# First chunks of the weight stream in another order: two modulation chunks ahead of the first query chunk

## What is computed

```
mod = silu(c) @ w_mod + b_mod                      # shift1, scale1, gate1, shift2, scale2, gate2
h   = rmsnorm(x, g_norm1) * (1 + scale1) + shift1  # c for latent tokens, c_ctx for context tokens
proj = h @ w_in + b_in                             # q, k, v, o, gates, pooling and branch gate columns
x  += gate1 * W_out(sig(g_a) * P_a(mLSTM(h)) + sig(g_b) * P_b(pool(h)))
x  += gate2 * HierMoE(h2)                          # 4 groups of 4 experts, top 1 group, top 2 experts
y   = rmsnorm(x, g_final)
```

## Time and profile before

| | us |
|---|---|
| median of 3 runs | 987.95 (986.37 to 990.32) |
| the profiled execution's own span | 983.7 |
| TensorE busy | 948.3 (96% of the span) |
| VectorE busy | 599.8 (61%) |
| ScalarE busy | 476.2 (48%) |
| GpSimd busy | 123.2 (13%) |

### The profile page before, as it was taken

One profiled execution on the slowest core, in us unless ns is written; L12 is line 12 of the kernel. 1 busy time (PEld: TensorE's weight loads), 2 busy tenths in 40 slices (PEclk: granted clock), 3 DMA queues, 4 the chain that ended last, 5 costly groups with the idle time before them and its releaser, 6 DMA issues.

```text
span 983.7 us, 13956 instructions
## 1 busy us (share of the span) xinstructions
PE 948.3 (96%) x5638; PEld 836.6 (85%) x5638; DVE 599.8 (61%) x767; ACT 476.2 (48%) x638; POOL 123.2 (13%) x133
## 2 busy tenths in 40 slices
PE   2999999999999999999999999989999999999986
PEld 1788888789999999999999998877888888888862
DVE  5353210234788862321344555459999999999998
ACT  5542121223566643122341242255878778787863
POOL 0000000001110029950000000002112111111100
PEclk9999999999999999999999999989999999999998
DMA  9835454713433253242212218148999999999964
GB/s 379 314 122 213 171 208 171 278 53 96 126 105 99 65 226 129 86 172 76 71 59 86 86 51 334 61 153 318 421 420 414 423 419 408 422 418 411 396 275 168
DMA packets 36192, 219.02 MB, mean 223 GB/s; under 512 B 3968, under 2 KB 4160, under 8 KB 15648
## 3 DMA queue, kind: packets, MB, share of 16 engines
q1 hardware_dynamic: 26496, 180.25, 46.5%
q0 software_dynamic: 8768, 35.15, 10.2%
q10 hardware_dynamic: 864, 2.73, 0.7%
HBM read 200.70 MB, written 17.42 MB: 222 GB/s over the span
## 4 chain that ended last, share of the span: by engine, by line
PE 90%; DMA 4%; DVE 4%; ACT 1%; issue 1%; SPq 0%; DVEq 0%; POOLq 0%; ACTq 0%
PE ps L1703 85%; PE ps L1759 2%; PE ps L2171 1%; DMA h2scr<-ht 1%; DMA xT<-in_x 1%; PE ps L2199 1%; DMA raw<-in_wst 1%; PE ps L1748 1%; DMA xg<-h2scr,slot_rows 0%; PE ps L2018 0%; PE ps L1911 0%; DVE rowA L1658 0%; DVE xr L1661 0%; DVE xr L1665 0%; DMA rowB<-yscr 0%
## 5 line engine op out<-in xcount | busy, mean ns | idle before, releaser
L1026 DVE TENSOR_TENSOR wlo<-raw,whi 128x2048 fp32r<-128x2048 f32 x29 | 67.5, 2327 | 158.4 <-ACT whi L633 158.4
L1703 PE MATMUL ps<-hhi,whi 128*128 128x320 f32 x672 | 155.5, 313 | 0.0
L1703 PE MATMUL ps<-hhi,wlo 128*128 128x320 f32 x672 | 153.1, 309 | 0.0
L1703 PE MATMUL ps<-hlo,whi 128*128 128x320 f32 x672 | 153.0, 309 | 0.0
L1703 PEld LDWEIGHTS ps<-hhi,whi 128*128 128x128 f32 x672 | 111.9, 188 | 11.3 <-ACT QK L680 5.9
L1703 PEld LDWEIGHTS ps<-hlo,whi 128*128 128x128 f32 x672 | 112.4, 188 | 0.0
L1703 PEld LDWEIGHTS ps<-hhi,wlo 128*128 128x128 f32 x672 | 112.3, 188 | 0.0
L633 ACT ACTIVATE whi<-raw 128x2048 fp32r<-128x2048 f32 x29 | 55.4, 1911 | 103.7 <-PE ps L1703 62.5
L1514 DVE TENSOR_TENSOR olo<-raw,ohi 128x2048 fp32r<-128x2048 f32 x32 | 72.4, 2288 | 3.9 <-ACT ohi L930 3.9
L1514 DVE TENSOR_TENSOR wlo<-raw,whi 128x2048 fp32r<-128x2048 f32 x31 | 70.3, 2289 | 5.0 <-ACT whi L930 4.7
L930 ACT ACTIVATE whi<-raw 128x2048 fp32r<-128x2048 f32 x32 | 61.3, 1918 | 18.8 <-PE ps L1703 18.8
(11 more groups left out here) (380 smaller groups left out, 1993.6 us busy)
## 6 DMA issues: line engine op xcount, KB each, us to landing
raw<-in_wexp SPq DMA_DIRECT2D x64, 1024.0 KB, 9.5
raw<-in_wst SPq DMA_DIRECT2D x60, 1024.0 KB, 5.1
eraw<-in_wexp SPq DMA_DIRECT2D x32, 1024.0 KB, 8.1
nm<-negscr POOLq DMA_DIRECT2D x8, 640.0 KB, 7.1
wib<-wiscr POOLq DMA_DIRECT2D x8, 512.0 KB, 6.2
xT<-in_x SPq DMA_DIRECT2D x4, 640.0 KB, 7.1
yscr<-zeros POOLq DMA_DIRECT2D x1, 2560.0 KB, 10.7
xr<-in_xt SPq DMA_DIRECT2D x1, 2560.0 KB, 9.9
```

What stands on the lines that cost most here:

```text
L1026: dve.tensor_tensor(lo[:, :], raw[s][:, :], f32(hi[:, :]), ALU.subtract)\
L1703: return nc.tensor.matmul(out, lhsT, rhs, start=start, stop=stop)
```

## The change

The order of the chunks in `wst` becomes: two modulation chunks, the query chunk, the other six modulation chunks. The query chunk thus has position and slot 2 (`AT_Q0`), and `m1_at` gives the position of modulation chunk i. ScalarE's high split of the query chunk goes from ahead of the inverse norm to behind the copy of the first modulation row; VectorE's low split goes from ahead of the normalising to behind the first gain, and there the low parts of blocks 0 and 1 go ahead of the normalising of blocks 4 and 5. On TensorE pair 1 goes from ahead of keys 0 to behind it, and turn 1 from ahead of keys 1 to behind it. Number, size and arithmetic of all products and transfers stay.

```diff
-AT_M1, AT_QK = 1, N_MOD1 + 1
+AT_Q0, AT_QK = 2, N_MOD1 + 1
+def m1_at(i):
+    return i if i < AT_Q0 else i + 1
...
             act.preload_act_table_set(LN_EXP)
-            split_hi(0, QH[0])
             act.wait_ge(s_ssq, 1)
             inv_rms(halves(rstd[:, :]), ps[:, 0:2, 0:HALF], D, s_rstd)
             for i in range(4):
-                chunk_used(act, AT_M1 + 2 * i + 1)
+                chunk_used(act, m1_at(2 * i + 1))
                 if i >= 2:
                     act.wait_ge(s_modT, i - 1)
                 act.activation(mrow1[:, i % 2, :], ps[:, 4, :], ACT.Copy).then_inc(s_mrow, 1)
+                if i == 0:
+                    split_hi(AT_Q0, QH[0])
                 act.wait_ge(s_gain, i + 1)
...
-            split_lo(0, QH[0], QL[0])
...
+                if i == 0:
+                    split_lo(AT_Q0, QH[0], QL[0])
+                    input_lo(0)
+                    input_lo(1)
                 if i < 2:
                     normalise(4 + 2 * i)
                     normalise(5 + 2 * i)
-                for k in (2 * i, 2 * i + 1):
-                    input_lo(k)
+                if i:
+                    for k in (2 * i, 2 * i + 1):
+                        input_lo(k)
...
-                mod_half(AT_M1 + 2 * i, 0, 4)
-                mod_half(AT_M1 + 2 * i + 1, 1, 4)
+                mod_half(m1_at(2 * i), 0, 4)
+                mod_half(m1_at(2 * i + 1), 1, 4)
...
             mod_pair(0)
             mod_turned(0)
-            mod_pair(1)
             pe.wait_ge(s_wgl, 1)
             pe.wait_ge(s_rstd, 1)
-            chunk_split(0)
+            chunk_split(AT_Q0)
             keys_outer(0)
+            mod_pair(1)
+            keys_outer(1)
             mod_turned(1)
-            keys_outer(1)
             mod_pair(2)
             keys_outer(2)
...
-    wst = np.concatenate([wq[0], wm1, ...
+    wst = np.concatenate([wm1[:AT_Q0], wq[0], wm1[AT_Q0:], ...
```

More of the change, by code:

```diff
@@ L117, in split_no @@
         return N_QK + 1 + c - AT_V
-    return (c - AT_QK) // 3 + 2 if c else 1
+    return (c - AT_QK) // 3 + 2 if c != AT_Q0 else 1
 def qk_at(j):
-    return AT_QK + 3 * (j - 1) if j else 0
+    return AT_QK + 3 * (j - 1) if j else AT_Q0
 def m2_at(g):
@@ L2321, in _layout @@
     wl = chunks(w[:, late], KT)
-    wst = np.concatenate([wq[0], wm1, np.concatenate([wq[1:], wm2[:-1]], 1).reshape(-1, P, CH), wv[:1], wm2[-1], wv[1:],
+    wst = np.concatenate([wm1[:AT_Q0], wq[0], wm1[AT_Q0:], np.concatenate([wq[1:], wm2[:-1]], 1).reshape(-1, P, CH), wv[:1], wm2[-1], wv[1:],
                           wl[:N_O],
```

## The result

The changed kernel takes 990.87 us in the median against 987.32 for the kernel before, measured beside each other (nine runs of each); the medians differ by 3.55. The ratio is 1.0042, with a 95% interval of 1.0030 to 1.0054, which is 4.1 us (3.0 to 5.3). The forecast was 991.2, or +3.26. A second measurement gave 1.0044 (1.0028 to 1.0060). So the change costs about 0.4%, which is within the 0.5% that were called "the same", and not within the noise of this many runs.

The account below looks back on a forecast made before the run. TensorE, busy 96% of the span, bounds the kernel; the opening pays for slot 0 and the fourth modulation chunk. Terms -0.54 + 0.34 + 1.86 + 1.60 give +3.26, so 987.95 becomes 991.2 us, range 987.9 to 994.0.

Parts of the forecast that it names:

- The prediction's own sign of being wrong: Keys 2 starting at 36 or earlier, or ends differing by more or less than the starts of keys 6.
- Part 1: First modulation row: pair done about 19.5 instead of 20.5, gain about 22.17 instead of 22.66, held by VectorE's normalising.
- Part 2: Query split behind the first row: low split 22.2 to 24.5, keys 0 at 25.4, 0.54 earlier than 25.94.
- The term -0.54: Earlier start of keys 0 on TensorE, 25.4 instead of 25.94, in us.
- Part 3: TensorE's order: pair 1 no longer hidden in the hole, 1.86 us; keys 2 waits a new 1.60 us.
- Part 4: Clock falls at 24.8, returns at 28.2; keys 0 takes 4.0 us, 0.34 more than before; bounds 2.74 and 4.95.
- the range stated for keys 0: Length of keys 0 between no half clock, 2.74 us, and half clock through all of it, 4.95.
- Part 5: Later modulation chunks cost nothing, hidden by keys 1 to 3; up to 4.9 us if that cover were gone.
- (a): Half clock through keys 0 (4.95) and pair 1 (2 x 1.56): +5.5, 993.4 us; chance 0.14.
- (b): The clock does not fall in the opening: +2.0, 989.9 us; chance 0.12.
- (c): Later TensorE waits give the lateness back, leaving only the 0.54 gained: 987.4 us; chance 0.08.
- (d): First row comes no earlier, held by sums or copy; keys 0 starts 0.5 later still: 991.7 us; chance 0.05.

Follow-up runs that it names:

- warm start: 15 products thrown away on TensorE ahead of the square sums: in the changed kernel with old TensorE order and holes filled, 1.0009; in the kernel before, 1.0009.
- the fillers: Products thrown away on TensorE: changed kernel with eight behind turn 0, 1.0037; with old order and holes filled, 1.0025; the latter with warm start, 1.0009; kernel before likewise, 1.0009.
- the kernel before with a warm start: Kernel before with products thrown away on TensorE, 15 ahead of the square sums and 2 inside pair 1; ratio 1.0009, median 988.5 us.
- the delay: Kernel before with 14 products of 128x256 thrown away on TensorE behind keys 7, a filler of 6.20 us; ratio 1.0086 to the kernel before.
- the first experiment: Changed kernel with TensorE's old order (pair 1 ahead of keys 0, turn 1 ahead of keys 1), chunks and splits as changed; ratio to the kernel before 1.0001.
- the new order alone: Kernel before with only TensorE's new order (keys 0, pair 1, keys 1, turn 1, pair 2), chunks and splits unmoved; ratio to the kernel before 1.0070.
- the two with fillers and new chunks: Changed kernel with TensorE's old order and products thrown away ahead of and inside pair 1, 1.0025; the same with 15 more before the square sums, 1.0009.

## Why the prediction was right

**The number.** The forecast of 991.2 lies 0.3 from the 990.87 measured, and part of that closeness is luck: its base, 987.95, was 0.6 above the 987.32 measured beside the changed kernel, and its difference, +3.26, is below the 3.55 of the medians and the 4.1 (3.0 to 5.3) of the ratio. The prediction's own sign of being wrong, ends that differ otherwise than the starts of keys 6, did not show in the first traces (3.2 against 2.98; keys 6 was forecast at 53.3 and began at 52.98). In the second ones the ends differ by 4.0 and the starts by 4.75; what separates them lies behind keys 6, where the kernel before alone differs by 3.15 between its two traces.

**Part 1, the first row.** Right in the first trace: copy at 19.43 (forecast 19.55), gain begun at 21.89 (the forecast had it done at 22.17). VectorE's normalising did hold it: it ran from 18.74 for 3.03 us, and the addition came behind it. What the forecast missed is that pair 0 does not always cost 1.48 + 1.07. In the six other traces with the new chunk order and no warm start it took 2.70 to 3.64, and the row's copy came between 19.9 and 21.0. With the old chunk order part of this is covered by the wait until the second chunk lands at about 19.4 (copy at 20.55, 20.56, 20.65 and 20.83 in four traces without a warm start); with the new one it is bare. So of the 1.1 us that the first trace shows at the copy, other executions keep 0.7 or less, and some nothing.

**Part 2, the splits.** Right: the low split ran from 21.96 to 24.2, block 0's low part behind it, keys 0 at 25.13 against 25.4. The term -0.54 measured -0.81 in the first traces, and +0.17 between the second (26.43 against 26.26).

**Part 3, the order.** Right, and the heart of it. Pair 1 took its 1.86 behind keys 0 (29.21 to 31.07), the chain from turn 1 to keys 2 was 4.26 against 4.27 forecast, and the new wait 1.47 against 1.60. At full clock the order costs 11.52 - 8.08 = 3.44, against the 1.86 + 1.60 = 3.46 of the sum, and the same in the kernel before without any other edit (11.53 - 8.08 = 3.45). Two single traces split it: 1.95 for the pair and 1.49 for the turn. Undone, the loss is gone (1.0001).

**Part 4, the clock.** Right for the first trace: 4.08 against the 4.0 forecast, +0.42 against +0.34. That thin work in the hole makes the clock fall is borne out by the fillers: it fell in all nine traces without them, between 22.1 and 24.7, and in none of the three with the new chunk order and the hole filled (keys 0 then took 2.67 to 2.74); the fourth with fillers, the kernel before with a warm start, did fall. The fall itself is not new with the change, for it stands in every trace of the kernel before. Of the range stated for keys 0 (2.74 to 4.95) the upper side occurred: 4.69 in the second trace of the changed kernel. With it keys 6 starts at 54.90, 4.75 behind the second trace of before, instead of 2.98. But those 4.75 are not the change alone: the opening of the kernel before was traced three times (the delay's edit lies behind it), each time with the clock back at about 28.1, while with TensorE's old order and the clock back at about 30.5 keys 0 took 4.53. How often either course of the clock comes in either kernel, no run tells. The forecast took the one of the first trace for the usual one, and whether that is why +3.26 lies below the measured difference stays open. The rule of the Trainium skill cited in the prediction ("TensorE: Matmul & The Clock Gate", "Part 1: The HAM clock gate"), that the throttled clock is the default and activity releases it, agrees with the trace: keys 0 begins at a granted clock of 0.50, after 4.00 us without a product.

**Part 5, transfers.** Right: the only idle time that the first trace names on TensorE from the hole to keys 7 is the wait for low parts (6.1 us in three waits, 4.0 of it the hole); no transfer appears.

**The rivals.** (a) came half true, in one traced execution of two, for keys 0 but not for pair 1, which took 1.85 there. Its price for the pair, twice 1.56, was too low besides: at half clock throughout one chunk takes 1.86 (24.45 to 26.31 in the first experiment), so a pair 3.7. (b) was not seen unless the hole was filled. (c) is refuted by the delay, and (d) by the first trace, though in the second the row was indeed no earlier.

**What stays open.** Four kernels (the new order alone, the delay, the two with fillers and new chunks) are 2.3 to 3.6 us slower in time than their openings against that of before say. The delay's 8.5 for 6.0 is the plainest. No trace shows where this lies: from keys 6 to the end, less the delay's filler, all thirteen traces take 933.7 to 936.9, and the upper end is the kernel before itself. All four were measured beside the same 17 runs of the kernel before, whose median, 986.06, is the lowest of four such groups (up to 987.32); a part may lie there, and no run separates it from a real cost. Falls of the clock behind the opening may be more frequent in these kernels; one trace of each can't tell. That lateness reaches the end whole is shown in one direction (nothing comes back), and not that nothing is added.

## What to carry to other kernels

Before a step is moved earlier, ask which product of the in-order engine was filling the hole in front of it, and where that product goes: here at most 1.1 us of earlier data were bought with 1.86 of work taken out of a hole and 1.5 of cover taken from the next row. The bare length of the chain that must be covered (4.27 here) could be read off the old trace, at the last row, where nothing covers it. The cost of the order was forecast from the distances between starts to a few hundredths of a microsecond (3.46 against 3.44); what could not be was the clock, which made keys 0 longer than in the kernel before by 0.4 us in one execution and by 1.0 in another. So read two traces before such a length is believed, and see where each traced execution stands among the runs.

## What the runs showed of the hardware

- The granted clock reads 1.00 from the start of the record, and is not to be believed there. The square sums take 2.47 us where TensorE was idle before and 1.34 where it had been kept busy since 4.77; pair 0, with both chunks landed, takes 2.31 to 3.64 under the same 1.00, against 1.92 for the same work in pair 2. In the first 20 us of these traces the durations of the products tell more of the clock than the row does.
- The time at which the clock falls and returns in the opening differs between executions of the same program: it was back near 28.1 in the first trace of the changed kernel and near 30.8 in the second. Over the other traces without fillers it came back at 28.1 (three traces of the old chunk and product order), and at 29.0, 29.4, 30.4 and 30.5.
- Filler products went with a held clock in three kernels, but such a start can also end badly: in the last kernel a wait of 1.33 us in front of pair 0's second chunk was followed by ten microseconds of half clock, through work that was dense from 22.1 on, and six of its twelve runs took 989.95 or more, against 987.0 or less for the rest.
- The same kernel takes 933.7 or 936.9 from keys 6 to the end in two executions, and 1.7 of that hang on whether the clock is at half in the tail near 960.
